# GpSimd takes a quarter of the weight splits of a mixture of experts, beside a router moved to the residual stream

## The reference, cut to what matters

```python
x = x + g1 * mix_x                                   # output projection, residual
h = _rmsnorm(x, norm2_g) * (1 + sc2) + sh2           # second norm, modulated
aff = softmax(h @ w_router)                          # (1024 tokens, 16 experts)
g, idx = top_k(aff.T, 128)                           # every expert chooses 128 tokens
# for each expert e, with x_e = h[idx_e]:
y_e = (silu(x_e @ w_gate[e]) * (x_e @ w_up[e])) @ w_down[e]      # 1024 -> 2816 -> 1024
x = x + g2 * zeros.at[idx_e].add(g_e * y_e)
out = _rmsnorm(x, final_g)
```

## Time and profile before

| what | value |
|---|---|
| median of 3 runs | 2657.16 us (2654.36 to 2657.73) |
| the profiled execution's own time | 2654.64 us |
| its span | 2652.8 us |
| mean granted clock of PE | 0.982 |
| busy: PE, DVE, ACT, POOL | 2534.7, 2111.9, 1475.8, 161.1 us |
| output projection and routing | about 955 to 1075 us |
| choice of tokens | about 1075 to 1115 us |
| experts and final norm | about 1115 to 2653 us |

### The profile page before, as it was taken

How to read it: one execution, slowest core, us unless ns; L and a number is a source line. 1 busy time by engine, 2 the same in 40 slices (tenths; PEclk the granted TensorE clock), 3 DMA queues, 4 the chain that set the end, 5 groups by cost and what they waited for, 6 DMA issues and landing times.

```text
span 2652.8 us, 31498 instructions
## 1 busy us (share of the span) xinstructions
PE 2534.7 (96%) x12267; PEld 2104.6 (79%) x12267; DVE 2111.9 (80%) x1974; ACT 1475.8 (56%) x1256; POOL 161.1 (6%) x177
## 2 busy tenths in 40 slices
PE   7999999999999999399999999999999999999996
PEld 3777889988888788288888888888888888888875
DVE  5775257688889565798989989988998898899886
ACT  4522247532111222277777777777777777777774
POOL 0011000001111000000000000000000000000011
PEclk9999999999999999599999999999999999999998
DMA  8799645554657632499999999999999999999994
GB/s 305 266 326 311 197 120 143 186 170 132 186 165 224 230 118 105 190 407 374 383 389 383 368 392 391 371 380 390 383 369 392 390 372 386 391 378 368 394 364 177
DMA packets 198050, 793.78 MB, mean 299 GB/s; under 512 B 17871, under 2 KB 65207, under 8 KB 127952
## 3 DMA queue, kind: packets, MB, share of 16 engines
q1 hardware_dynamic: 164132, 693.67, 69.3%
q0 software_dynamic: 32464, 96.50, 11.8%
q10 hardware_dynamic: 1310, 1.64, 0.3%
HBM read 719.64 MB, written 67.91 MB: 297 GB/s over the span
## 4 chain that ended last, share of the span: by engine, by line
PE 51%; issue 4%; DMA 2%; DVE 1%; ACT 0%; POOL 0%; POOLq 0%; DVEq 0%; ACTq 0%
PE moe_ps_gate L2396 18%; PE moe_ps_y L2386 17%; PE moe_ps_up L2396 14%; PE moe_ps_h L2367 1%; DMA acc_d<-moe_y,idx_col 1%; DMA moe_over_lo<-acc_d 1%; PE moe_ps_x L2357 0%; DMA out<-moe_over_lo 0%; DVE moe_w_lo L2486 0%; ACT moe_w_hi L2429 0%; DMA moe_xe<-h_d,idx_col 0%; DVE moe_ht_lo L2520 0%; ACT moe_discarded L2459 0%; ACT moe_discarded L2466 0%; DVE raw L2529 0%
## 5 line engine op out<-in xcount | busy, mean ns | idle before, releaser
L2486 DVE TENSOR_TENSOR moe_w_lo<-raw,moe_w_hi 128x2048 fp32r<-128x2048 f32 x528 | 1207.6, 2291 | 162.1 <-ACT moe_w_hi L2429 158.4
L2429 ACT ACTIVATE moe_w_hi<-raw 128x2048 fp32r<-128x2048 f32 x528 | 1012.0, 1919 | 404.3 <-PE moe_ps_gate L2396 145.4
L2396 PE MATMUL moe_ps_gate<-moe_w_hi,moe_xt_hi 128*128 128x512 f32 x768 | 303.0, 395 | 1.0 <-DVE moe_xt_lo L2477 1.0
L2396 PE MATMUL moe_ps_gate<-moe_w_hi,moe_xt_lo 128*128 128x512 f32 x768 | 299.6, 390 | 0.0
L2396 PE MATMUL moe_ps_gate<-moe_w_lo,moe_xt_hi 128*128 128x512 f32 x768 | 299.2, 390 | 0.0
L2396 PE MATMUL moe_ps_up<-moe_w_hi,moe_xt_hi 128*128 128x512 f32 x640 | 255.3, 399 | 0.0
L2396 PE MATMUL moe_ps_up<-moe_w_hi,moe_xt_lo 128*128 128x512 f32 x640 | 250.1, 391 | 0.0
L2396 PE MATMUL moe_ps_up<-moe_w_lo,moe_xt_hi 128*128 128x512 f32 x640 | 249.4, 390 | 0.0
L2386 PE MATMUL moe_ps_y<-moe_w_hi,moe_ht_hi 128*128 128x512 f32 x704 | 219.1, 393 | 14.8 <-DVE moe_ht_lo L2520 14.8
L2386 PE MATMUL moe_ps_y<-moe_w_hi,moe_ht_lo 128*128 128x512 f32 x704 | 218.6, 392 | 0.0
L2386 PE MATMUL moe_ps_y<-moe_w_lo,moe_ht_hi 128*128 128x512 f32 x704 | 218.6, 392 | 0.0
(11 more groups left out here) (315 smaller groups left out, 3698.4 us busy)
## 6 DMA issues: line engine op xcount, KB each, us to landing
raw<-in_w_moe SPq DMA_DIRECT2D x528, 1024.0 KB, 7.3
hyena_g_parts<-gw_d POOLq DMA_DIRECT2D x64, 512.0 KB, 4.7
proj_w_mod<-in_w_mod SPq DMA_DIRECT2D x32, 512.0 KB, 6.8
gw_d<-proj_g_parts POOLq DMA_DIRECT2D x16, 1024.0 KB, 7.3
w_in<-in_w_in SPq DMA_DIRECT2D x12, 1024.0 KB, 8.6
attn_table<-in_na_table SPq DMA_DIRECT2D x16, 576.0 KB, 5.5
norm_w_mod<-in_w_mod SPq DMA_DIRECT2D x16, 512.0 KB, 10.8
proj_g_raw<-in_w_in SPq DMA_DIRECT2D x16, 512.0 KB, 10.0
```

What stands on the lines that cost most here:

```text
L2396: mm = pe.matmul(ps, hp[:, e % 2, k, :], wp[:, r, :], start=(k == 0 and x == 0), stop=(k == KD - 1 and x == 2))
L2429: act.activation(w_hi[:, g % PARTS], raw[:, g % RAW], ACT.Copy).then_inc(hi_ready, 1)
L2486: dve.tensor_tensor(w_lo[:, g % PARTS], raw[:, g % RAW], w_hi[:, g % PARTS].bitcast(F32), ALU.subtract).then_inc(lo_ready, 1)
```

## The change

There are three parts.

- **POOL makes low parts.** Every unit g from 8 to 461 with g % 4 == 2 is split by POOL instead of DVE, into the same slot by the same subtraction, and counted in `lo_by_pool`. PE, SP and POOL wait by `wait_lo`. POOL does the splits of an expert between a gather and the scatter. The last two experts' units stay with DVE.
- **Router on the residual stream.** The tile that is turned and routed is x1 before the norm, with the router scaled by (1 + sc2) * norm2_g (`scaled`); the inverse root comes onto the logits behind, and the shift's share of the logits (`shift_e`) is made once by eight matmuls and added. The columns for this are loaded in rows and turned. The loops over tiles are written out; the last tile's matmuls are done in two halves of columns with turns and routes between. The softmax is made up to the affinities in project_out. The last tile's h2 is made in choose by ACT and POOL. The copy of the turned affinities goes: the first round reads PSUM.
- **The last expert.** Tiles 3 to 7 have places in raw slots 0 to 2 and are loaded without waiting for a store; squares come later (AT+19 instead of AT+16 for the first; AT is the step of the last expert's first unit). POOL multiplies by the gain once a tile is squared, and DVE (six tiles) or ACT (two) multiplies by the inverse root. The last weight unit's matmuls are done in two halves of columns, each counted, so that DVE can start on the first half.

The core of the diff:

```diff
@@ project_out, tensor @@
-                def turn(t, s):
-                    pe.wait_ge(normed, t + 3)
+                def turn(t, ks, last_half=False):
+                    pe.wait_ge(x1_ready, t + 1 + last_half)
...
+                out(0)
+                pe.wait_ge(cols_in, 4 * 16)
+                pe.transpose(ps_cols, col_rows[:], ident[0:3 * KD, 0:3 * KD]).then_inc(router_steps, 1)
+                out(1)
+                pe.wait_ge(router_steps, SHIFT_SPREAD)
+                for k in range(KD):
+                    mm = pe.matmul(ps_e, shift_w[:, k, :], router[:, k, :], start=(k == 0), stop=(k == KD - 1))
+                mm.then_inc(router_steps, 1)
+                turn(0, every)
+                for t in range(2, LAST):
+                    out(t)
+                    turn(t - 1, every)
+                    route(t - 2, every)
+                may_project(LAST)
+                for k in range(KD):
+                    mm = step(LAST, 0, k)
+                    if k == KD // 2 - 1:
+                        route(LAST - 2, every)
+                mm.then_inc(projected, 1)
+                turn(LAST - 1, every)
+                for k in range(KD):
+                    mm = step(LAST, 1, k)
+                    if k == KD // 2 - 1:
+                        route(LAST - 1, every)
+                        turn(LAST, low)
+                mm.then_inc(projected, 1)
+                route(LAST, low)
+                turn(LAST, high, True)
+                route(LAST, high, True)
@@ choose @@
+            @block.gpsimd
+            def _(pool):
+                pool.wait_ge(last_row_steps, UNIT_LAST)
+                pool.tensor_tensor(last, last, scale_row[:], ALU.mult).then_inc(last_row_steps, 1)
+                pool.wait_ge(last_row_steps, GAINED_LAST)
+                pool.tensor_tensor(last, last, shift_row[:], ALU.add).then_inc(last_row_steps, 1)
...
-                dt.then_wait(dve.tensor_copy(rows[:], ps_r[0:2 * E_N, :]))
@@ experts @@
+        POOL_UNITS = [g for g in range(RAW, N_ALL - 2 * N_U) if g % 4 == 2]
+        BY_POOL = {g: n + 1 for n, g in enumerate(POOL_UNITS)}
+        def wait_lo(eng, g):
+            if g in BY_POOL:
+                eng.wait_ge(lo_by_pool, BY_POOL[g])
+            else:
+                eng.wait_ge(lo_ready, g + 1 - sum(p < g for p in POOL_UNITS))
...
-        SQUARE = {AT + 16: 0, AT + 17: 1, AT + 18: 2, AT + 26: 3, AT + 27: 4, AT + 28: 5, AT + 30: 6, AT + 31: 7}
-        SCALE = {AT + 20: 0, AT + 21: 1, AT + 22: 2, AT + 33: 3, AT + 34: 4, AT + 35: 5, AT + 36: 6, AT + 37: 7}
+        SQUARE = {AT + 19: 0, AT + 20: 1, AT + 22: 2, AT + 30: 3, AT + 31: 4, AT + 32: 5, AT + 33: 6, AT + 34: 7}
+        ROOT = {AT + 24: 0, AT + 35: 1}
+        SCALE = {AT + 26: [0], AT + 27: [1], AT + 28: [2], AT + 36: [3, 4, 5]}
+        SCALE_ACT = {AT + 36: [6, 7]}
...
+                def split(g):
+                    pool.wait_ge(hi_ready, g + 1)
+                    if g >= PARTS:
+                        pool.wait_ge(used, g - PARTS + 1)
+                    pool.tensor_tensor(w_lo[:, g % PARTS], raw[:, g % RAW], w_hi[:, g % PARTS].bitcast(F32),
+                                       ALU.subtract).then_inc(lo_by_pool, 1)
...
+                    for g in POOL_UNITS:
+                        if g <= until_scatter(e) and (e == 0 or g > until_scatter(e - 1)):
+                            split(g)
                     pool.wait_ge(y_ready, e + 1)
...
+                def gain_of(t):
+                    pool.wait_ge(squared, t + 1)
+                    pool.tensor_tensor(x[t], x[t], gain[:], ALU.mult).then_inc(gained, 1)
...
-                for t in range(3):
-                    pool.wait_ge(tile_out[t], 16)
-                    load(t + 3)
...
+                        if (e, u) == (LAST_E, CARRIED):
+                            for n in range(2):
+                                cols = slice(n * 512, (n + 1) * 512)
+                                for f in range(2):
+                                    ht = [x[:, c % 2, f, :] for x in (ht_hi, ht_lo)]
+                                    for x, (hp, wp) in enumerate(((ht[0], hi), (ht[0], lo), (ht[1], hi))):
+                                        mm = pe.matmul(ps_y[:, cols], hp, wp[:, f, cols], start=False, stop=(f == 1 and x == 2))
+                                mm.then_inc(used, 1)
+                            return
...
-                    if AHEAD <= g < N_ALL:
+                    if AHEAD <= g < N_ALL and g not in BY_POOL:
                         split(g)
...
-                        dve.scalar_tensor_tensor(out=x[t], in0=x[t], scalar=inv[:, t:t + 1], in1=gain[:],
-                                                 op0=ALU.mult, op1=ALU.mult).then_inc(out_ready, 1)
+                        dve.wait_ge(gained, t + 1)
+                        dve.tensor_scalar(x[t], x[t], inv[:, t:t + 1], None, ALU.mult).then_inc(out_ready, 1)
```

More of the change, by code:

```diff
@@ L1920, in store @@
[L1920 to L1931, removed]
@@ L1943, in out, with step @@
-                def out(t, s, first=False):
-                    pe.wait_ge(m_split, t + 3)
-                    pe.wait_ge(x1_ready, t + 1)
+                def step(t, n, k):
+                    for x, (h, w) in enumerate(((m_hi, w_hi), (m_hi, w_lo), (m_lo, w_hi))):
+                        mm = pe.matmul(ps_o[:, t % 2, n * 512:(n + 1) * 512], h[t % 2][:, k, :],
+                                       w[k // 4][:, k % 4, n * 512:(n + 1) * 512], start=(k == 0 and x == 0),
+                                       stop=(k == KD - 1 and x == 2))
+                    return mm
@@ L1971, in _ @@
-                out(0, 0, first=True)
-                pe.wait_ge(rows_in, 5 * 16)
-                out(1, 1)
-                turn(0, 0)
-                with pe.Fori(0, TT // 2 - 1) as i:
-                    for s in range(2):
-                        out(2 * i + s + 2, s)
-                        turn(2 * i + s + 1, 1 - s)
-                        route(2 * i + s, s)
-                turn(TT - 1, 1)
-                route(TT - 2, 0)
-                route(TT - 1, 1)
+                        for n in range(2):
+                            mm = step(t, n, k)
@@ new lines, in _ @@
+                every, low, high = range(KD), range(KD // 2), range(KD // 2, KD)
+                out(0)
[6 more added lines that the diff above has]
+                mm.then_inc(router_steps, 1)
@@ new lines, in _ @@
+                for t in range(LAST):
+                    act.wait_ge(x1_ready, t + 1)
+                    act.activation(squares[:], x1[:, t % 2], ACT.Square, accum_out=ss[:, t:t + 1]).then_inc(squared, 1)
+                    rooted_of(t)
+                    act.wait_ge(turned, t + 1)
+                    if t == 1:
+                        act.wait_ge(router_steps, SHIFT_TURNED)
+                    if t >= 2:
+                        act.wait_ge(routed, t - 1)
+                    act.activation(x1_t[:, t % 2].rearrange("p k q -> p (k q)"), ps_h[:], ACT.Copy).then_inc(copied, 1)
@@ L2103, in unit_view, with choose @@
     return slot.rearrange("p (r n) -> p r n", r=2 if name == "down" else KD // parts)
-def choose(nc, sems, a, keep, logits, raw, raw_in, gate_col, idx_col):
+def choose(nc, sems, a, keep, halves, raw, raw_in, gate_col, idx_col):
     ident = keep["ident"]
@@ L2627, in program @@
             raw_in = [sems(f"raw_in{s}") for s in range(RAW)]
-            choose(nc, sems, a, keep, logits, raw, raw_in, gate_col, idx_col)
+            choose(nc, sems, a, keep, halves, raw, raw_in, gate_col, idx_col)
         experts(nc, sems, a, keep, raw, raw_in, gate_col, idx_col, out)
```

332 lines of the change are left out of this document (199 added, 133 removed).

## The result

The changed kernel takes 2762.55 us (median of 4 runs, 2761.88 to 2765.79), the kernel before 2655.76 us on the same chip (2652.02 to 2657.73): ratio 1.0404 [1.0388, 1.0419], slower. Forecast: 2745, range 2628 to 2805. The time is 17.6 us above the forecast. That a size is nearly right doesn't mean that its working is, and here one step of it isn't.

What follows compares the result with a forecast made beforehand. PE was taken to bound the experts before the change, DVE experts 0 to 13 after it. From 2654.6 us, 113 for GpSimd's splits, less 6.2 (router) and 16.4 (last expert), gave 2745, range 2628 to 2805.

Steps and rivals of the forecast that it cites:

- PE bounds the experts, relief of DVE is worth nothing: Experts' steady stage: PE busy 100.00 of 100 us, DVE 90, so the 259 us of work DVE saves gain nothing.
- GpSimd's price, 2 x 2.29 = 4.58 us: Weight splits on GpSimd: two inputs brought in one after the other take twice DVE's 2.29 us; ends 2.29 and 6.87.
- Exclusion, read from gathers that end 0.85 us after a split: Experts: GpSimd's read waits while DVE runs an instruction with two SBUF inputs, and DVE's split waits for GpSimd's whole 4.58 us.
- DVE then sets the pace of the experts 0 to 13: Experts 0 to 13: DVE exceeds PE's pace by 1.0 us per four units, a loss of 113 us.
- The sum of 12.3 us for four units: Experts, four units: DVE's 7.9 us plus GpSimd's 4.58, less about 0.2, against PE's 11.3.
- second way to pay: Experts: a held split ahead of the hidden layer's low part stops PE, five times an expert; up to 0.5 us per four units.
- the row of 0.88 us of room: Hidden layer's way back: DVE ends its low part at 1706.59, PE starts the down unit with it at 1707.47.
- Router, 6.2 us: Last projection tile to search: transposes 5.5 us sooner, and a dropped copy of 0.68 us; ends 3 and 8 us.
- Last expert, 16.4 us: Last expert: 15 of 18.2 us lost to stops and lower clock regained, plus 1.4 us at the end.
- late next: Last expert: three GpSimd gains of 2.3 us among DVE's splits may stop the low part 1 us each; ACT squares 1.06 us.
- The sum: Whole kernel: 2654.6 + 113 - 6.2 - 16.4 = 2745 us.
- What would show it: Changed profile: longer or gapped DVE splits, GpSimd's at 4.5 us or more, PE below 95 of 100, gathers near 101 us apart.

Runs made afterwards that it cites:

- the run that reads: DVE makes all low parts; at the changed kernel's 113 GpSimd units, GpSimd does two unused 128x1024 subtractions with both inputs in SBUF: 2852.22 us, ratio 1.0746.
- the one that only writes: DVE makes all low parts; at the changed kernel's 113 GpSimd units, GpSimd does four 128x1024 memsets that read nothing: 2645.33 us, ratio 0.9968.
- the tight run: Changed kernel, but GpSimd splits only units 9, 16, 22 and 30 of an expert, 56 in all: 2772.02 us, ratio 1.0438 against the kernel before.

## Why the prediction was right in its time, and wrong in one step

**PE bounds the experts, relief of DVE is worth nothing.** Right. Without GpSimd's splits PE is at 100 in the steady stage; with 55 of them, DVE's count of splits 55 lower, the time is the same (2644.66 and 2645.32).

**GpSimd's price, 2 x 2.29 = 4.58 us.** Right: 4.62 free, in the mean 4.81. The Trainium skill's 4497 ns ("GPSIMD Engine Reference", section 3.1) is 3% below.

**Exclusion, read from gathers that end 0.85 us after a split.** Right, shown by the run that reads and the one that only writes. It works both ways: POOL's 4.62 becomes 5.61 where a split of DVE is first, and gathers take up to 2.58 us.

**"DVE then sets the pace of the experts 0 to 13", 113 x 1.0 us.** This is the step that failed. The sum of 12.3 us for four units took it that GpSimd's whole 4.58 us comes on top of DVE's work. DVE is held less: (2873 - 2310) ns x 415 / 113 = 2.1 us a unit, since part of GpSimd's split falls into time in which DVE waits for its next high part anyway (1.8 us of delay beside a split of 4.63, above). That gives 7.9 + 2.1 = 10.0 us of 11.3, no saturation; the windows above had DVE at 77 and 79 of 100. The loss came by the "second way to pay", which the forecast called "mostly the same loss told twice" and kept at up to 0.5 us in the range: with PE's stops (85.5 us) and the longer matmuls (34.2) it accounts for all of the 119.7 us in the experts. That 113 and 117.2 are close is chance: with the same count, other places give 33 to 188 us. Where the row of 0.88 us of room stood in the argument, I should have asked which units come before it.

**Router, 6.2 us.** Right, if it is counted from the projection's own start. Timelines of the changed kernel, to be held against the earlier trace rows:

```profile
955.85 0.47 PE L1951 MATMUL out_ps_o<-out_w_hi,out_m_hi 128*128 128x512 f32 x1 [0.56 <-PEq L1736]
...
1050.21 0.48 PE L1951 MATMUL out_ps_o<-out_w_hi,out_m_hi 128*128 128x512 f32 x1
...
1066.43 0.69 DVE L2069 TENSOR_TENSOR out_x<-out_ps_o,out_g_row 128x512 f32<-128x512 f32 x1 [2.05 <-PE out_ps_o L1951]
...
1072.76 1.01 PE L2245 MATMUL choose_ps_r<-identity,out_halves 128*32 128x128 f32 x4 [2.45 <-PEq L1914]
...
1107.64 0.21 DVE L2265 CAST choose_where_f<-choose_where 32x128 f32<-32x128 uint32 x1
```

The kernel before starts the projection at 954.79:

```profile
954.79 0.70 PE L1951 MATMUL out_ps_o<-out_w_hi,out_m_hi 128*128 128x512 f32 x2 [1.01 <-ACTq L1987]
```

From there to the transposes it is 122.44 us before and 116.91 after, 5.5 less as forecast, and 6.25 less to the last cast, with the copy gone. Seen from the last tile's first matmul the transposes come 7.8 us sooner (22.55 us for 30.35); that matmul stands 2.3 us later in the projection, where I had allowed 2.2. But the whole projection starts 1.1 us later, so on the clock of the execution only 4.5 us are left at the transposes. The runs with the changed kernel's router start it between 954.3 and 959.6 us and need 116.8 to 118.7 us to the transposes. What moves the start isn't settled, as there is one profile of the kernel before. In the run without splits the start is at 956.08, and the transposes (1074.62) come 2.6 us sooner than before.

**Last expert, 16.4 us.** Mis-sized, and by the item that was named as "late next". Three gains were to stop the low part by 1 us each; the stop is 6.17 us after the change and 6.44 without splits, and a stop of 3.8 us for the last product is new in both. So of 13.4 us of stops 10.0 are still there. From the gather for expert 15 to the end the change gains 7.4 us; without splits 199.6 us for 205.7, 6.1; with the gains back on DVE 194.0, 11.7. The same exclusion whose price I had worked out for the experts I took at a third of it here: two gains held DVE's three splits by 5.8 us, 2.9 each. ACT's waits for tiles that hadn't landed did go, from 13.2 us to 2.1.

**The sum** by what was measured, 2655.6 + 117.2 - 10.3 = 2762.5, closes by construction, as both terms are taken from the run without splits. The error of 17.6 is 12.3 of gains that didn't come, 4.2 of loss above the forecast and 1.0 between the medians and the profiled execution.

**What would show it.** 415 splits at a mean far above 2.29, GpSimd's above 4.5 us, gathers 101.8 us apart in the mean from 1239.07 to 2562.26 (forecast 101, before 93.3), PE at 100 again in expert 14: all seen. PE is below 95 in one of the two windows shown. The gathers were forecast at one distance and came at four; that was the sign of place over sum. The transposes were forecast 5 to 6 us sooner after the start of the last tile and come 7.8 sooner. "PE busy over 90 of the last 103" failed: it is 79.06 (2657.6 to 2760.6), before 73.80.

## What to carry to other kernels

Before work moves from DVE to GpSimd, count whether both would read SBUF with DVE at two inputs; then the question isn't whether the sums fit but what stands on DVE's queue behind each held instruction, and how soon it is wanted, and what stands ahead of the moved one on GpSimd's. 55 splits at slack places were free, 56 at tight ones cost 127 us. Don't pick moved units by a count that drifts through the loop (every fourth of 33). And relief of an engine that isn't the bound brought nothing even where it was free.

## What the runs showed of the hardware

- GpSimd's subtraction of 128x2048 fp32 with both inputs in SBUF takes 4.62 us, DVE's 2.29; a multiplication or addition of 128x1024 takes GpSimd 2.33 us.
- Such a subtraction and DVE's split take turns whole: three splits in 12.67 us for 6.9 with two gains between, two in 13.64 for 4.5. Operations of DVE with an input in PSUM keep their duration (128x512, hidden low part 681 ns, product 676 ns; before 684 and 681).
- GpSimd's memsets, 452 of 952 ns, don't touch DVE: 2311 ns a split against 2310.
- A stop of PE costs more than its length. After 7.83 us the pair of matmuls takes 1.19 us for 0.62. Behind stops of 0.96 and 0.97 us in the tight run it takes 0.70. In the experts of the changed kernel 85.5 us of stops came with 34.2 us of longer matmuls.
